# Entry of the state-mixing layer: first mix moved ahead of the wide low-rank sums, low-rank rows regrouped over tiles 1 to 3, slab 5 split ahead of the third mix, key fans one tile later

## What is computed

```
xx = h_prev - h
xr, xw, xk, xv, xa, xg = (h + xx * mu[i] for i in range(6))
r, k, v = xr @ w_rkv[0], xk @ w_rkv[1], xv @ w_rkv[2]
w_log = -softplus(-(w0 + tanh(xw @ w1) @ w2)) - 0.5
a = sigmoid(a0 + (xa @ a1) @ a2)
g = sigmoid(xg @ g1) @ g2
kk = (k * k_k) / norm_per_head(k * k_k)
k = k * (1 + (a - 1) * k_a)
```

## Time and profile before

| what | value |
|---|---|
| median of 3 runs | 1652.77 us (1652.15 to 1655.19) |
| the profiled execution | 1655.15 us |
| its span, first to last instruction | 1653.2 us |
| PE busy | 1609.4 us, 97% |
| DVE / ACT / POOL busy | 1137.8 / 841.4 / 711.1 us |
| mean granted clock of TensorE | 0.997 |
| the touched stage | about 376 to 519 us of the span |

### The profile page before, as it was taken

The page is one execution under the profiler, slowest core; times in us unless marked ns, Lnnn a source line. Parts: engine busy times, 40 slices in busy tenths (PEclk is TensorE's granted clock), DMA queues, the critical chain, the costliest instruction groups (busy, mean ns, idle before and its releaser), DMA issues.

```text
span 1653.2 us, 36557 instructions
## 1 busy us (share of the span) xinstructions
PE 1609.4 (97%) x13805; PEld 1537.0 (93%) x13805; DVE 1137.8 (69%) x1989; ACT 841.4 (51%) x1593; POOL 711.1 (43%) x695
## 2 busy tenths in 40 slices
PE   8989999999999999999999999999999999999998
PEld 8879999997898999999999877999999878999997
DVE  6967777537587567777755766777765796777743
ACT  5465555534653333555543474566533464655533
POOL 5644666200065211466611351466611764566500
PEclk9999999999999999999999999999999999999999
DMA  5415556453230004555455321555445513555443
GB/s 188 163 52 147 149 145 166 137 149 104 82 123 8 11 4 135 153 146 144 138 147 172 118 80 51 151 152 152 136 140 159 154 53 102 153 146 145 133 143 105
DMA packets 331820, 203.97 MB, mean 123 GB/s; under 512 B 7816, under 2 KB 327448, under 8 KB 331584
## 3 DMA queue, kind: packets, MB, share of 16 engines
q1 hardware_dynamic: 329200, 195.45, 41.0%
q0 software_dynamic: 1776, 5.60, 1.0%
q10 hardware_dynamic: 736, 1.41, 0.2%
HBM read 198.95 MB, written 3.39 MB: 122 GB/s over the span
## 4 chain that ended last, share of the span: by engine, by line
PE 79%; DVE 8%; POOL 5%; ACT 4%; issue 3%; DMA 1%; SPq 0%; DVEq 0%; POOLq 0%; ACTq 0%
PE bank L980 22%; PE bank L982 22%; PE bank L981 22%; PE bank L1438 4%; DVE lo L2349 2%; ACT hi L1785 2%; POOL lo L688 1%; PE bank L992 1%; PE bank L1366 1%; DVE SC L2566 1%; POOL qsin L708 1%; PE bank L1337 1%; PE bank L1034 1%; POOL K L766 1%; PE bank L966 1%
## 5 line engine op out<-in xcount | busy, mean ns | idle before, releaser
L980 PE MATMUL bank<-XH,hi 128*128 128x320 f32 (+1 forms) x1912 | 599.0, 313 | 2.6 <-issue 1.2
L2349 DVE TENSOR_TENSOR lo<-raw,hi 128x2048 fp32r<-128x2048 f32 (+2 forms) x193 | 408.3, 2116 | 271.1 <-ACT hi L1785 271.1
L982 PE MATMUL bank<-XH,lo 128*128 128x320 f32 (+1 forms) x1912 | 590.7, 309 | 0.0
L981 PE MATMUL bank<-XL,hi 128*128 128x320 f32 (+1 forms) x1912 | 590.7, 309 | 0.0
L1785 ACT ACTIVATE hi<-raw 128x2048 fp32r<-128x2048 f32 (+2 forms) x201 | 352.1, 1752 | 74.1 <-PE bank L982 65.4
L980 PEld LDWEIGHTS bank<-XH,hi 128*128 128x128 f32 (+1 forms) x1912 | 358.7, 188 | 12.6 <-issue 7.2
L981 PEld LDWEIGHTS bank<-XL,hi 128*128 128x128 f32 (+1 forms) x1912 | 358.8, 188 | 1.3
L982 PEld LDWEIGHTS bank<-XH,lo 128*128 128x128 f32 (+1 forms) x1912 | 358.7, 188 | 0.0
L737 POOL TENSOR_TENSOR upad<-upad,rpad 128x656 f32<-128x656 f32 x88 | 147.7, 1678 | 204.3 <-ACT upad L1906 204.3
L980 PE MATMUL bank<-GH,hi 128*128 128x320 f32 x704 | 218.6, 311 | 1.8 <-DVE lo L2349 1.8
L741 POOL COPY ust<-upad 128x4 f32 (+1 forms) x176 | 214.1, 1247 | 13.5 <-POOL upad L737 13.0
(11 more groups left out here) (396 smaller groups left out, 2317.0 us busy)
## 6 DMA issues: line engine op xcount, KB each, us to landing
raw<-in_f_w_up SPq DMA_DIRECT2D x176, 512.0 KB, 5.0
raw<-in_f_w_down SPq DMA_DIRECT2D x64, 704.0 KB, 4.7
raw<-in_b_w_rkv SPq DMA_DIRECT2D x12, 1024.0 KB, 5.1
raw<-in_a_w_in SPq DMA_DIRECT2D x11, 1024.0 KB, 5.6
raw<-in_a_w_out SPq DMA_DIRECT2D x8, 1024.0 KB, 5.2
raw<-in_b_w_out SPq DMA_DIRECT2D x4, 1024.0 KB, 6.1
raw<-in_c_w_out SPq DMA_DIRECT2D x4, 1024.0 KB, 5.2
raw<-in_a_w_in SPq DMA_DIRECT2D x6, 512.0 KB, 4.5
```

The costliest lines, as they stand in the source:

```text
L980: pe.matmul(out, a, xh(k), start=(start and k == 0), stop=False)
L981: pe.matmul(out, a, xl(k), start=False, stop=False)
L982: last = pe.matmul(out, b, xh(k), start=False, stop=(stop and k == kt - 1))
L2349: dve.tensor_tensor(lo[n % 2][:, 0:w_], raw[n % 2][:, 0:w_], hi[n % 2][:, 0:w_].bitcast(F32), ALU.subtract).then_inc(w_lo, 1)
```

## The change

- The spare tile and an early Tanh on ACT load the tanh table at the stage's beginning.
- DVE doesn't mix xg between the norm halves. It makes the first mix at once, and after it mixes xg into VV (not K). PE's wide sums run behind product 0, into bank 4 (not 6), and are evacuated by ACT after tile 0.
- The 24 rows are regrouped by ROWS_AFTER: three pairs (m = 0 to 2, a = 0, 1) ahead of product 0, then 7, 6 and 5 rows behind products 1, 2 and 3, with all a = 2 behind product 1 or later. A row waits for the evacuation of the row of the same a two tiles before. ACT rounds tiles 2 to 7 of the first mix between the first six evacuations, and the second mix behind the evacuations of each group.
- In product 0 the fillers (2) stand ahead of tiles 5 to 7 only; four stand ahead of the first rows.
- ACT splits slab 5 right after tile 7; the third mix is cut 5 and 3, with slab 6's split between the parts on ACT and on DVE.
- The key fans run behind products 13, 14 and 15 (before 12, 13, 14). The eight fillers ahead of product 10 are gone.

```diff
+        ROWS_AFTER = {-1: [(m, a) for m in range(3) for a in range(2)],
+                      1: [(m, a) for m in (3, 4) for a in range(2)] + [(m, 2) for m in range(3)],
+                      2: [(m, a) for m in (5, 6) for a in range(2)] + [(m, 2) for m in (3, 4)],
+                      3: [(7, a) for a in range(2)] + [(m, 2) for m in (5, 6, 7)]}
...
-                    for k in tiles:
-                        pe.wait_ge(lora_mix, 9 * z + 6 + k % 4)
-                        low_rank(6, L1, wide, K, k, opens=k == 0, closes=k == KD - 1)
                 pe.wait_ge(shift_set, 1)
-                pe.transpose(psum[3][0:16, 0:128], sho[:, :], ident).then_inc(shift_turned, 1)
+                pe.transpose(psum[1][0:16, 0:128], sho[:, :], ident).then_inc(shift_turned, 1)
+                keep(4, 7)
+
+                def wide_low_rank():
+                    for k in range(KD):
+                        pe.wait_ge(lora_mix, 11 + k)
+                        low_rank(4, L1, wide, VV, k, opens=k == 0, closes=k == KD - 1)
+
+                def low_rank_rows(i):
+                    for m, a in ROWS_AFTER[i]:
...
+                        if m >= 2:
+                            pe.wait_ge(lora_evac, ROW_AT[m - 2, a])
...
+                low_rank_rows(-1)
...
-                fans_at = {12: (0, 1), 13: (2, 3, 4), 14: (5, 6, 7)}
+                fans_at = {13: (0, 1), 14: (2, 3, 4), 15: (5, 6, 7)}
...
-                    if i == 10:
-                        keep(8, 6)
...
-                        if i == 0:
-                            keep(2 if k else 6, 7)
+                        if i == 0 and k > 4:
+                            keep(2, 7)
...
-                    if i < 4:
-                        lora_rows(2 * i)
-                        lora_rows(2 * i + 1)
+                    if i == 0:
+                        wide_low_rank()
+                    elif i < 4:
+                        low_rank_rows(i)
...
+                act.wait_ge(still_set, 1)
+                act.activation(spare[:, :], still[:, 0:1], ACT.Tanh)
...
+                highs(0, 0, 2)
                 middle(0)
-                high(0, 0)
                 middle(1)
+                for z, (m, a) in enumerate(ROWS_AFTER[-1]):
+                    high(0, 2 + z)
+                    low_rank_row(m, a)
...
+                tile(0)
                 middle(2)
+                highs(1, 0, 2)
+                tile(1)
+                for m, a in ROWS_AFTER[1]:
+                    low_rank_row(m, a)
+                split_hi(s0 + 2)
+                highs(1, 2, 4)
+                tile(2)
+                for m, a in ROWS_AFTER[2]:
+                    low_rank_row(m, a)
+                highs(1, 4, 6)
+                tile(3)
+                for m, a in ROWS_AFTER[3]:
+                    low_rank_row(m, a)
+                split_hi(s0 + 3)
+                highs(1, 6, 8)
...
                 tile(7)
+                split_hi(s0 + 5)
                 key_squares(6)
                 key_squares(7)
-                highs(2, 0, 4)
-                split_hi(s0 + 5)
+                highs(2, 0, 2)
                 tile(8)
-                highs(2, 4, 8)
-                key_roots(1)
+                highs(2, 2, 5)
                 tile(9)
                 split_hi(s0 + 6)
+                highs(2, 5, 8)
+                key_roots(1)
...
                 for z in range(2):
                     normed(z)
-                    for k in range(4 * z, 4 * z + 4):
-                        mixed(K[:, k, :], k, 5).then_inc(lora_mix, 1)
...
                 mix(0, 0, 8)
+                for k in range(KD):
+                    mixed(VV[:, k, :], k, 5).then_inc(lora_mix, 1)
                 split_lo(s0 + 1)
-                dve.wait_ge(lora_mid, 1)
+                dve.wait_ge(lora_mid, 2)
...
-                mix(2, 0, 4)
                 split_lo(s0 + 5)
-                mix(2, 4, 8)
+                mix(2, 0, 5)
+                split_lo(s0 + 6)
+                mix(2, 5, 8)
...
                 decays(0, 3)
-                split_lo(s0 + 6)
                 inverse(1)
```

More of the change, by code:

```diff
@@ L265, in build @@
         still = sb("still", [128, 128])
+        spare = sb("spare", [128, 1])
         over = base[0]
@@ L489, in build @@
         cqn_done, lat_parts, kc_rope, latf_done, head_roped = map(sem, "cqn_done lat_parts kc_rope latf_done head_roped".split())
+        ROWS_AFTER = {-1: [(m, a) for m in range(3) for a in range(2)],
+                      1: [(m, a) for m in (3, 4) for a in range(2)] + [(m, 2) for m in range(3)],
+                      2: [(m, a) for m in (5, 6) for a in range(2)] + [(m, 2) for m in (3, 4)],
+                      3: [(7, a) for a in range(2)] + [(m, 2) for m in (5, 6, 7)]}
+        ROW_AT = {row: z + 1 for z, row in enumerate(row for i in (-1, 1, 2, 3) for row in ROWS_AFTER[i])}
         CHUNKS = 5
@@ L1345, in pe_rwkv @@
                     for k in tiles:
-                        pe.wait_ge(lora_mix, 9 * z + k % 4 + 1)
+                        pe.wait_ge(lora_mix, 5 * z + k % 4 + 1)
                         low_rank(4, L1, narrow, HN, k, opens=k == 0)
-                    pe.wait_ge(lora_mix, 9 * z + 5)
+                    pe.wait_ge(lora_mix, 5 * z + 5)
                     for k in tiles:
                         low_rank(4, L1X, narrow, XX, k, closes=k == KD - 1)
-                    for k in tiles:
-                        pe.wait_ge(lora_mix, 9 * z + 6 + k % 4)
-                        low_rank(6, L1, wide, K, k, opens=k == 0, closes=k == KD - 1)
                 pe.wait_ge(shift_set, 1)
-                pe.transpose(psum[3][0:16, 0:128], sho[:, :], ident).then_inc(shift_turned, 1)
[L1357 to L1364, removed]
+                pe.transpose(psum[1][0:16, 0:128], sho[:, :], ident).then_inc(shift_turned, 1)
[6 more added lines that the diff above has]
+                    for m, a in ROWS_AFTER[i]:
+                        if i < 0 and m == 0 and a == 0:
+                            pe.wait_ge(lora_in, 96)
+                            pe.wait_ge(lora_act, 2)
+                        if m == 0 and a == 2:
+                            pe.wait_ge(lora_act, 3)
+                        if m >= 2:
+                            pe.wait_ge(lora_evac, ROW_AT[m - 2, a])
                         r_ = (slice(0, 64), slice(64, 128), slice(0, 128))[a]
@@ L1398, in pe_rwkv @@
                         pe.wait_ge(rkv_evac, i - 1)
+                    if i == 1:
+                        pe.wait_ge(shift_out, 1)
                     xh, xl = ((XH, XL), (XH2, XL2), (XH, XL))[j]
                     def mixed(k):
-                        if i == 0:
-                            keep(2 if k else 6, 7)
+                        if i == 0 and k > 4:
+                            keep(2, 7)
                         pe.wait_ge(mix_done, KD * j + k + 1)
@@ L2092, in middle, with low_rank_row @@
                     act.wait_ge(lora_mid, 1 + a // 2)
-                    act.activation((LTg if a == 2 else LT)[r_, :], psum[4 + a // 2 * 2][r_, 0:T], (ACT.Tanh, ACT.Copy, ACT.Sigmoid)[a]
+                    act.activation((LTg if a == 2 else LT)[r_, :], psum[4][r_, 0:T], (ACT.Tanh, ACT.Copy, ACT.Sigmoid)[a]
                                    ).then_inc(lora_act, 1)
[L2096 to L2103, removed]
+                def low_rank_row(m, a):
+                    act.wait_ge(lora_out, ROW_AT[m, a])
+                    ps = psum[(2, 5)[m % 2] + a][:, 0:T]
+                    if a < 2:
+                        act.activation((LW, A)[a][:, m, :], ps, ACT.Sigmoid, bias=vcol(("b_w0", "b_a0")[a], m)).then_inc(lora_evac, 1)
+                    else:
+                        act.copy(G[:, m, :], ps).then_inc(lora_evac, 1)
                 def tile(i):
@@ L2126, in gate_scale @@
                     act.activation(G[:, m, :], G[:, m, :], ACT.Copy, scale=vcol("b_ln_w", m)).then_inc(gate_done, 1)
+                highs(0, 0, 2)
                 middle(0)
-                high(0, 0)
                 middle(1)
-                middle(2)
[L2132 to L2141, removed]
+                for z, (m, a) in enumerate(ROWS_AFTER[-1]):
+                    high(0, 2 + z)
+                    low_rank_row(m, a)
+                act.wait_ge(shift_turned, 1)
+                act.copy(shot[:, :], psum[1][0:16, 0:128]).then_inc(shift_out, 1)
+                tile(0)
+                middle(2)
+                highs(1, 0, 2)
[13 more added lines that the diff above has]
+                highs(1, 6, 8)
                 tile(4)
@@ L2623, in normed @@
                         ins.then_inc(lora_mix, 1)
-                    dve.wait_ge(lora_mix, 9 * z + 4)
+                    dve.wait_ge(lora_mix, 5 * z + 4)
                     chain(dve.tensor_tensor(XX[:, k_, 1:T], HN[:, k_, 0:T - 1], HN[:, k_, 1:T], ALU.subtract))
@@ L2627, in normed @@
                     dve.tensor_scalar(XX[:, k_, 64], HN[:, k_, 64], -1.0, None, ALU.mult).then_inc(lora_mix, 1)
```

(2 more changed lines are left out.)

## The result

The change made the kernel slower by 0.21%: median 1657.54 us of 20 runs (1655.09 to 1663.04) against 1654.97 us of 20 runs of the kernel before (1651.49 to 1658.64), ratio 1.0021 with a 95% interval of 1.0013 to 1.0029. That is 2.2 to 4.8 us. The forecast was +1.6 us and "no measurable change"; the time lies in the range and the sum had the right sign, but the loss can be told from no change (the interval is 0.08% to either side, 1.3 us, where the prediction took 0.2%, 3.3 us), and a slower kernel had a chance of 0.22. The means are 1658.13 and 1654.73 us, 3.4 apart. A second set of 11 runs gave 1.0023 (1.0011 to 1.0035).

What follows compares the result with a forecast made beforehand. PE at 97% busy was taken as the bound, with the chain over ACT, POOL and DVE from 467 us on. Entry -1.4, third mix and fans +2.4, clock +0.6 gave +1.6 us: 1654.4 us, range 1650.0 to 1658.3.

Steps and rivals of the forecast that it cites:

- the clock term: At the new PE idle of 3.4 us ahead of product 14: a likely drop to 1.2 GHz costs 0.6 us, bounds 0 to 1.7.
- The entry: From first mix to product 4: earlier mix and moved wide sums gain 1.7 us, 1.4 after row losses; bounds 0.3 to 2.5.
- The rows behind: Rows behind products 1 to 3: fewer form changes but waits for bank copies, 9.1 against 8.85 us, a loss of 0.25.
- The third mix and the fans: Third mix to stage end: PE's gains given back, later scans and fans end the stage 2.4 us later; bounds 1.1 to 5.7.
- The scans: DVE's scans after the third mix: end at 468.2 instead of 467.09, so the Exp chain starts 1.1 us later.
- the last head: Head 7 on DVE, behind the later key fans: ends at 485.4, 5.7 us later than before.
- DVE's waits for ACT: DVE behind head 7: 2.9 us of idle for ACT's slab splits vanishes and absorbs part of the lateness.
- ahead by 2.3 us: PE in the third mix: its lead from the missing filler and slab 6 wait, before waiting for tiles 10 and 12.
- three signs of being wrong: Product 4 over 2.5 us earlier, no PE gap at product 14, or the last head sum earlier than 518.
- 1: Stage end: late fans not absorbed, all 5.7 us stay and the clock costs 1.7; +6.0 us, 1658.8; chance 0.20.
- 2: Whole stage: PE sets the end, so filler, slab wait and entry gains arrive; -3.7 us, 1649.1; chance 0.13.
- 3: Stage end: POOL sets it, fans lie under its chain, only Exp's 1.1 counts; -0.3 us, 1652.5; chance 0.20.

Runs made afterwards that it cites:

- third_only: The kernel before with only the change's third mix, slab order, fans and missing fillers; ratio 1.0020 to the kernel before.
- both_filled: The changed kernel with four fillers ahead of the third pair of rows and 15 ahead of product 14; ratio 1.0001 to the kernel before.
- fans_back: The changed kernel with the key fans behind products 12, 13 and 14 again; ratio 1.0013 to the kernel before.
- gap_filled: The changed kernel with 15 fillers (3.2 us) on PE ahead of product 14; ratio 1.0007 to the kernel before.
- entry_only: The changed kernel with third mix, slab order, fans and the fillers ahead of product 10 as before; ratio 0.9995 to the kernel before.
- entry_filled: The changed kernel's entry alone, rest as before, plus four fillers on PE ahead of the third pair of rows; ratio 1.0000 to the kernel before.
- the two kernels with fillers: The changed kernel with entry fillers, and either 15 ahead of product 14 (1.0001) or fans behind products 12 to 14 with twelve ahead of fan 2 (1.0002).

## Why the prediction was wrong in size

**The step that failed is the clock term**, +0.6 us with bounds 0 and 1.7. By the difference of means it came to about 2.3 us (3.4 less the 1.06 at full clock). The term counted one place only, the gap ahead of product 14, and took a third of its price. A drop there cost 1.47 us in the changed kernel (95.35 against 93.88 with the gap filled), because it delayed the fans behind product 14 and with them head 7 (by 1.54 us). It came in all four profiles with an unfilled gap there or ahead of the fans, in two of them with double length (third_only 96.04, 2.16 us above 93.88, which is over the bound of 1.7), and in none of the three of the whole third-mix order with fillers. And a second place wasn't in the sum at all: behind the row pairs of the entry with their 0.88 us wait the clock fell in three of five profiles and cost 1.54 us (47.81 against 46.27); with four fillers it fell in none of five. I had treated that wait as time alone. That the low clock makes the changed kernel's distance from its +1.06 us is shown by both_filled, in the profile and by time.

How the loss divides between the two places is less sure. Three drops in five profiles against none in five can be chance: three drops fall by luck on the unfilled half in 1 of 12 cases. And the sets of runs show the gap ahead of product 14, but not the wait in the entry. With the gap open the mean clock lay below that of before beside it (third_only 0.9949 and fans_back 0.9939 against 0.9960); with it filled and the entry's wait open (gap_filled 0.9959), or in entry_only (0.9961), it did not, and entry_filled, with its wait filled, lay lower than before (0.9957 against 0.9967). How often the clock falls in the entry stays open.

**The entry**: forecast -1.4, measured -1.06 at full clock. Product 1 came 1.36 us earlier in entry_only, not 1.7. On the time scale of the kernel before, product 0 started 0.5 us later than worked out (397.09 with the stage 0.19 earlier, so 397.28), but product 1 only 0.1 later (406.31 against 406.2), since product 0 and the wide sums together took 0.4 us less than worked out. The larger part of the miss is the point of comparison: the prediction had 407.9 for before, and product 1 began there at 407.67. The rows behind lost 0.3, forecast 0.25.

The Trainium skill, "ScalarE: Activation LUTs", section "What ACT_TABLE_LOAD costs", has 1.38 us of drain with a table load. The timeline of ACT in the changed kernel doesn't show it:

```profile
394.44 1.28 ACT L2116 ACT_TABLE_LOAD   x1
395.73 0.53 ACT L2116 ACTIVATE AR<-bank,V 128x320 f32<-128x320 f32 x1
```

**The third mix and the fans**: forecast +2.4 behind the entry, measured +2.10. The scans were 1.25 late (forecast 1.1), the last head 5.9 us at full clock (forecast 5.7; in both_filled it starts 57.97 us behind product 4, before 52.04), and DVE's waits for ACT vanished as said. From head 7 to the last head sum DVE took 35.91 us in both_filled and 39.74 before: 2.87 of the difference are the waits that the timeline names (forecast 2.9), and 0.96 is shorter work (forecast 0.4). The second isn't as simple as the sum had it. Three of DVE's splits behind head 7 now start while POOL is at work and take 2.96 us each (before 2.29, 2.29 and 2.44), and other DVE work is shorter by more than that. The late fans cost 0.87, for which the sum had 1.3.

**Luck and slips.** The two terms at full clock add up to +1.04 measured and +1.0 forecast, but that is luck: the entry gained 0.34 less than forecast and the rest lost 0.3 less. Two steps of the prediction don't come out as written: 459.8 + 2.16 + 2.4 + 3.6 is 468.0 and not 468.2 for the scans, and a PE "ahead by 2.3 us" needs the filler row's whole 1.95 us, where the text takes 1.7 (with 0.34, 2.0). Both are small beside the clock. None of its three signs of being wrong came, so they could not have found this error.

**The rivals**: 1 had a price for the clock of 1.7 and expected head 7's lateness unabsorbed; its clock half was nearer than the forecast's 0.6, the other half was wrong (3.8 of 5.9 us were absorbed). 2 fell with third_only. 3, only the later scans count, fell with both_filled: 2.10 us at full clock, where they lost 1.25.

With the clock term at 2 to 3 us in place of 0.6 the same sum would have given +3 to +4.

## What to carry to other kernels

Where an edit opens a wait on PE, price it twice: its length, and a drop of the clock behind it, which cost 1.5 to 2.2 us here and came now and then behind a wait of 0.9 us next to half-array work too. Put filler into such a wait: in both places here it cost nothing. Moving a split ahead of DVE work paid here where little waiting for the split's other half, on ACT, came with it (slab 5), and not where it brought a new wait (slab 6); a wait in the middle of a chain was passed on whole, while a late branch was mostly absorbed by idle time behind it (late fans moved head 7 by 4.7 us, 57.97 against 53.28 in the two kernels with fillers, and the end by 0.9).

## What the runs showed of the hardware

Behind a wait of 0.88 us among row products on half arrays the clock fell in three of five executions of the same instructions. A kernel's times go with its mean clock: in one set of the changed kernel 0.990 to 0.998 goes with 1665.16 to 1655.20 us. Not all of this is the touched stage, since the profiles also show drops outside it, with and without the change (before at 1372.6 us, the changed kernel at about 650 us).

Two pairs of half-array products in a row took 1.27 us (start to start, 412.24 to 413.51 in the changed kernel). A pair runs at once in 0.54, so that leaves 0.2 for the change of form, as the rounds of before suggested.

DVE's split of a slab took 2.29 us where it started just before a product of POOL, which then took 2.9 instead of 0.87, and up to 3.0 where it started during one.
